# Up-projection of a conv feed-forward block: every product in three split products, with GpSimd making three quarters of the low weights

## Chip, core and metric

The kernel runs on one core of a Trainium2 chip. The metric is the device time of one launch in microseconds (us). All data are fp32. The core's engines are named as the profile names them: PE is TensorE (matmul), PEld its weight loads, DVE is VectorE, ACT is ScalarE, POOL is GpSimd, SP is the engine that issues most of the transfers.

## What is computed

The program is one block of a network on 256 tokens with 1024 features, followed by two layers of a second kind. The change is in the feed-forward part of the first block, in its up-projection:

```python
def conv_ffn(h, w_up_l, w_dwc_l, w_down_l, on_grid):
    p = h @ w_up_l                                  # 256 x 1024 times 1024 x 5632
    val, gate = p[..., :D_FF], p[..., D_FF:]        # D_FF = 2816
    ...
        gate = lax.conv_general_dilated(gate.reshape(bsz, rows, GRID_W, D_FF), w_dwc_l[:, :, None, :], ...)
    ...
    return (jax.nn.silu(gate) * val) @ w_down_l
```

The convolution is depthwise with nine taps on a 4 x 64 grid of tokens.

## The kernel before

Weights come as a stream of chunks of 128x2048 numbers (1 MB), chunk n into slot n % 4 of `raw`. A product with full accuracy is made of three fast ones (`mm3`): a number is split into a high part (rounded to the type fp32r) and a low part (the number less its high part), and high x high, low x high and high x low are summed in PSUM. ACT makes the high weights (`w_hi`, by a copy), DVE the low ones (`w_lo`, by a subtraction of `w_hi` from `raw`), both double-buffered by n % 2.

The up-projection has 22 chunks (N_UP = 14 to 35), each the weights of one block of 128 features: the first 1024 columns of a chunk make the value half, the last 1024 the gate half. A step of the stage is one chunk, and `up_chunk` (L445) is PE's part of it. Its value half is eight plain fp32 products of `raw` and `h_up` (L450; the profile counts each as two MATMULs), its gate half is 8 x 3 split products (L397 to L399). So only the gate half needs `w_hi` and `w_lo`. The order of the work is written out by hand on every engine, with semaphores:

- PE waits for `lo_ready` of the chunk and for a free PSUM bank (`evicted`; four banks, so PE may be up to three chunks ahead), and raises `chunk_done`.
- ACT (`up_steps` from L1374): copies the gate half out of PSUM twice (`gpad` L1378, `gacc` L1380), raises `gate_in`, makes the high gate weights of the chunk two further on (`prep`, 128x1024 from L1109), then a tanh of the chunk before (L1395) and the high part of the gated result of two chunks before (`mid_hi` L1400).
- DVE (`up_steps`): eight taps of the convolution (L2087), each waiting for the one before it, and between them two low-weight pieces of 512 columns (L2097) after the second and third tap, `mid_lo` (L2059), and the two steps of silu times value (L2064, L2069; the second reads the value half in PSUM and raises `evicted`). The ninth tap is in ACT's `gacc`.
- In the last two steps all 2048 columns of the first down-projection chunks are prepared, in four DVE pieces.
- GpSimd issues transfers of other weights (L362) and does nothing else.

Before the first chunk, DVE, ACT and PE go through the eight blocks of the normalised input: DVE scales (L2048), ACT adds the shift into `h_up` (L1370) and copies its high part (L1372), DVE subtracts (L2049).

Of the kernel before, what the change touches and what calls it, by code (L numbers as in the profile page):

```python
# [16 lines left out]
P = 128  # L17
D = 1024
KT = D // P
# [71 lines left out]
def build_program(nc, io, layers=LAYERS):  # L91
# [6 lines left out]
    with ctx:  # L98
# [9 lines left out]
        def at(name, shape, offset, dt=f32):  # L108
            return nc.alloc_sbuf_tensor_at(name, shape, dt, offset=offset)
# [51 lines left out]
        def S(name):  # L161
            if name not in sems:
                sems[name] = ctx.enter_context(nc.semaphore(name))
            return sems[name]
# [78 lines left out]
        mod_rows = at("mod_rows", [P, CH], F[0])  # L243
        ada_first = [ada_f[:, i, :] for i in range(4)] + [ada_a[:, i, :] for i in range(3)] + [ada_6[:, 0, :]]
        y1 = at("y1", [P, KT, T], A[5])
        h_up = at("h_up", [P, KT, T], F[2])

        mid_hi1 = at("mid_hi1", [P, FB, T], A[0], f32r)
        mid_lo1 = at("mid_lo1", [P, FB, T], A[0] + FB * T * 4, f32r)
# [103 lines left out]
        @block.gpsimd  # L353
        def _(pool):
            pool.wait_ge(S(f"ada_first{ADA_FIRST - 1}"), 16)

            def load(i, free=None):

                for c in range(2):
                    if free is not None:  # L360
                        pool.wait_ge(S("ada_used"), 2 * free + c + 1)
                    pool.dma_start(ada_home(i, c), io["ada"][2 * i + c + ADA_FIRST]).then_inc(ada_sem(i, c), 16)  # L362
            load(0)
            for i in range(1, 15):
                load(i, i - 1)
            load(15, 13)
            load(16, 14)
            load(17, 15)
            load(18, 16)
            pool.wait_ge(S("chunk_done"), N_DOWN)  # L370
            load(19, 17)
            load(20, 18)
            pool.wait_ge(S("chunk_done"), N_LAYER)
            load(21, 19)
            pool.wait_ge(S("gated"), 12)
            load(22, 20)
            load(23, 21)
            load(24, 22)
            load(25, 23)
            load(26, 24)  # L380
            pool.wait_ge(S("chunk_done"), N_LAYER + L_WOUT + 4)
            load(27, 25)
            load(28, 26)
            load(29, 27)
            pool.wait_ge(S("gated"), 24)
            load(30, 28)
            load(31, 29)
# [5 lines left out]
        def _(pe):  # L393
            mm, tr = nc.tensor.matmul, nc.tensor.transpose

            def mm3(out, ah, al, bh, bl, first, last, shared=False):
                mm(out, ah, bh, start=first, stop=False, skip_group_check=shared)  # L397
                mm(out, ah, bl, start=False, stop=False, skip_group_check=shared)  # L398
                return mm(out, al, bh, start=False, stop=last, skip_group_check=shared)  # L399
# [42 lines left out]
                                   act_hi[s][:, k, :], act_lo[s][:, k, :], k + b == 0, k == KT - 1, shared=True)  # L442
                return last

            def up_chunk(wp, slot, bank, m=None):  # L445

                for k in range(KT):
                    if m is not None:
                        pe.wait_ge(S("up_h"), k + 1)
                    mm(ps[:, bank, 0:T], raw[:, slot, k * P:(k + 1) * P], h_up[:, k, :], start=k == 0, stop=k == KT - 1)  # L450
                for k in range(KT):
                    if m is not None:
                        pe.wait_ge(S("mod_lo"), 8 * m + k + 1)
                    o = (KT + k) * P
                    last = mm3(ps[:, bank, T:2 * T], w_hi[:, wp, o:o + P], w_lo[:, wp, o:o + P],
                               act_hi[1][:, k, :], act_lo[1][:, k, :], k == 0, k == KT - 1)
                return last

            def tok_chunk(wp, bank, s):
# [425 lines left out]
            def up(i, m):  # L885
                for c in range(m):
                    first = isinstance(i, int) and i == 0
                    pe.wait_ge(S("lo_ready"), i + (N_UP + c + 1))
                    pe.wait_ge(S("evicted"), J_UP if first else i + (J_UP + c - 3))
                    more = {"m": 2} if first and c == 0 else {}  # L890
                    up_chunk((N_UP + c) % 2, (N_UP + c) % RAW, c % 4, **more).then_inc(S("chunk_done"), 1)
            up(0, 4)
            with pe.Fori(1, FB // 4) as i:
                up(i * 4, 4)
# [199 lines left out]
        def _(act):  # L1094
# [270 lines left out]
            root(2)  # L1365
            prep(N_OUT1 + 5, (N_OUT1 + 5) % RAW, (N_OUT1 + 5) % 2)
            norm_x(3, x, norm_sq1, 1)
            for b in range(KT):
                act.wait_ge(S("mod_pre"), 16 + b + 1)
                act_(h_up[:, b, :], norm_h1[:, b, :], ACT.Identity, bias=mod[:, 24 + b:25 + b]).then_inc(S("up_h"), 1)  # L1370
                act.wait_ge(S("up_h"), b + 1)
                act_(act_hi[1][:, b, :], h_up[:, b, :], ACT.Copy).then_inc(S("mod_hi"), 1)  # L1372

            def up_steps(i, c):  # L1374

                n, s, e, first = N_UP + c, c % 2, i + c, isinstance(i, int) and i == 0
                act.wait_ge(S("chunk_done"), i + (n + 1))
                act_(gpad[:, s, 1:ROWS + 1, 1:GRID_W + 1],  # L1378
                     ps[:, c % 4, T:2 * T].rearrange("p (r w) -> p r w", r=ROWS), ACT.Copy)
                act_(gacc[:, c, :], ps[:, c % 4, T:2 * T], ACT.Copy, scale=vec[:, bass.ds(e + (V1["dwc"] + 4 * FB), 1)])\  # L1380
                    .then_inc(S("gate_in"), 1)
                if isinstance(i, int):
                    prep(i + n + 2, (i + n + 2) % RAW, (i + n) % 2, CH // 2 if i + c + 2 < FB else 0)
                else:
                    prep((i + (n + 2), i * (16 // RAW) + ((n + 2) // RAW * 16 + 16)), (n + 2) % RAW, n % 2, CH // 2)
                if not (first and c == 0):
                    up_tanh(i, c)
                if not (first and c < 2):
                    up_mid(i, c)

            def up_tanh(i, c):

# [4 lines left out]
            def up_mid(i, c):  # L1397

                act.wait_ge(S("evicted"), i + (J_UP + c - 1))
                act_(mid_hi1[:, bass.ds(i + (c - 2), 1), :], gm[:, c % 2:c % 2 + 1, :], ACT.Copy).then_inc(S("mid_hi"), 1)  # L1400
# [242 lines left out]
        def _(dve):  # L1643
# [383 lines left out]
            for hf in (1, 0):  # L2027
# [18 lines left out]
            prep(N_UP + 1, (N_UP + 1) % RAW, (N_UP + 1) % 2)  # L2046
            root_done(3)
            pipe(2, lambda b: stt(norm_h1[:, b, :], x[:, b, :], gs[:, 1, b:b + 1], rstd[:, :], ALU.mult, ALU.mult),  # L2048
                 lambda b: tt(act_lo[1][:, b, :], h_up[:, b, :], act_hi[1][:, b, :].bitcast(f32), ALU.subtract))  # L2049
            nc.vector.memset(gpad[:, :, :, :], 0.0).then_inc(S("cleared"), 1)  # L2050
            order(nc.vector.memset(sw_wide[:, :, 8:16], 0.0))
            base = order.n
# [18 lines left out]
            def up_steps(i, c):  # L2071


                n, s, e, first = N_UP + c, c % 2, i + c, isinstance(i, int) and i == 0
                order.n = base if first and c == 0 else i * UP_MARKS + (base + c * UP_MARKS - 1)
                w_slot, r_slot = n % 2, (n + 2) % RAW
                gate_only = not isinstance(i, int) or i + c + 2 < FB
                pieces = {1: 1024, 2: 1536} if gate_only else {1: 0, 2: 512, 3: 1024, 4: 1536}
                dve.wait_ge(S("gate_in"), e + 1)
                acc = gacc[:, c, :].rearrange("p (r w) -> p r w", r=ROWS)  # L2080
                silu_mark = None
                for at_, tap in enumerate((0, 1, 2, 3, 5, 6, 7, 8)):
                    src = gpad[:, s, tap // 3:tap // 3 + ROWS, tap % 3:tap % 3 + GRID_W]
                    w = vec[:, bass.ds(e + (V1["dwc"] + tap * FB), 1)]
                    if at_:
                        dve.wait_ge(S("dve_order"), tap_mark)
                    ins = stt(acc, src, w, acc, ALU.mult, ALU.add)  # L2087
                    if at_ < 7:
                        order.mark(ins)
                        tap_mark = order.n  # L2090
                    else:
                        ins.then_inc(S("gconv"), 1)
                    if at_ in pieces:
                        if at_ == 1:
                            dve.wait_ge(S("hi_ready"), i + (n + 3))
                        o = slice(pieces[at_], pieces[at_] + 512)
                        ins = tt(w_lo[:, w_slot, o], raw[:, r_slot, o], w_hi[:, w_slot, o].bitcast(f32), ALU.subtract)  # L2097
                        if pieces[at_] == 1536:
                            ins.then_inc(S("lo_ready"), 1)
                    if at_ == 4 and not (first and c < 2):  # L2100
                        up_lo(e, s)
                    if not (first and c == 0):
                        if at_ == 5:
                            up_silu_a(e, 1 - s, (c + 3) % 4)
                            silu_mark = order.n
                        if at_ == 6:
                            up_silu_b(1 - s, (c + 3) % 4, silu_mark)
# [38 lines left out]
            for L in range(layers):  # L2146
# [265 lines left out]
                for hf in range(2):  # L2412
# [14 lines left out]
                        prep(n + c + 2, (n + c + 2) % RAW, (n + c) % 2)  # L2427
                        mlp_steps(0, c)
                    mlp_steps(0, 7)
                    prep_halves(n + 9, 2 * L + hf + 1)  # L2430
                    if hf == 1:
                        mods_out()
                    if hf == 0:
# [151 lines left out]
```

## Time and profile before

| | |
|---|---|
| Median of 3 runs | 1735.22 us (1732.3 to 1739.69) |
| The profiled execution: its own time | 1738.21 us |
| The profiled execution: span from the first to the last instruction | 1736.4 us |
| PE busy | 1648.1 us, 95% |
| DVE busy | 1108.8 us, 64% |
| ACT busy | 813.8 us, 47% |
| POOL busy | 34.0 us, 2% |

The engines work side by side, and busy times of matmuls overlap each other, so a busy PE is not PE at its peak. The shares are means over stages with different limits; the stage of the change lies between 327 and 482 us of the span.

### The profile page before, as it was taken

What the parts mean: (1) busy time and instruction counts of PE and PEld (TensorE: products, weight loads), DVE (VectorE), ACT (ScalarE), POOL (GpSimd) and SP (SyncE); (2) the same over time, 40 slices, a digit from 0 to 9 for tenths busy, and PEclk for the clock granted to TensorE, in tenths of its full rate; (3) what the DMA queues carried; (4) which work ended last, traced back from release to release, by engine and by line L of the source; (5) the groups of instructions that cost most, each with busy time, mean ns of one, the idle gap of its engine ahead of it and who ended that gap; (6) DMA issues with size and microseconds to landing.
All of it is one profiled execution on the core that took longest, in us unless ns stands there. A gap on an engine that the chain in (4) does not pass through costs nothing.

```text
span 1736.4 us, 34270 instructions
## 1 busy us (share of the span) xinstructions
PE 1648.1 (95%) x15182; PEld 1570.4 (90%) x15182; DVE 1108.8 (64%) x1400; ACT 813.8 (47%) x1057; POOL 34.0 (2%) x68
## 2 busy tenths in 40 slices
PE   5998999999998999999998999999999999989997
PEld 4996888799996999999997999979999999979996
DVE  3577744788946464678867545565546877665464
ACT  3346324433334536458544435444544675445352
POOL 0001000000000000000001000000000000000000
PEclk8999999999998999999999999999999999999998
DMA  9437444744546546445558655554454545735552
GB/s 390 159 123 264 151 178 180 269 166 165 203 175 229 170 147 194 157 170 182 173 193 346 235 189 194 188 208 171 151 189 146 195 170 175 267 117 193 193 189 81
DMA packets 45529, 331.40 MB, mean 191 GB/s; under 512 B 5072, under 2 KB 5072, under 8 KB 5456
## 3 DMA queue, kind: packets, MB, share of 16 engines
q1 hardware_dynamic: 36032, 260.73, 43.6%
q0 software_dynamic: 9216, 67.11, 9.9%
q8 instruction: 113, 1.85, 0.4%
q10 hardware_dynamic: 144, 1.51, 0.2%
q14 instruction: 24, 0.20, 0.0%
HBM read 326.18 MB, written 1.05 MB: 188 GB/s over the span
## 4 chain that ended last, share of the span: by engine, by line
PE 74%; DVE 12%; ACT 8%; DMA 4%; issue 2%; SPq 1%; POOL 0%; ACTq 0%; DVEq 0%; POOLq 0%
PE ps L397 19%; PE ps L399 19%; PE ps L398 19%; DVE w_lo L1652 5%; PE ps L450 4%; ACT w_hi L1109 4%; DMA raw<-stream 2%; PE ps L525 2%; DMA ada_alt<-ada 1%; PE ps L693 1%; PE ps L682 1%; DVE rsq L2420 1%; DMA ada_raw<-ada 1%; DVE rstd L1699 1%; PE ps L501 1%
## 5 line engine op out<-in xcount | busy, mean ns | idle before, releaser
L397 PE MATMUL ps<-act_hi,w_hi 128*128 128x256 f32 x2672 | 756.7, 283 | 17.6 <-DVE act_lo L1728 4.6
L1652 DVE TENSOR_TENSOR w_lo<-raw,w_hi 128x2048 fp32r<-128x2048 f32 x207 | 474.4, 2292 | 448.9 <-ACT w_hi L1109 448.3
L398 PE MATMUL ps<-act_lo,w_hi 128*128 128x256 f32 x2672 | 747.6, 280 | 0.0
L399 PE MATMUL ps<-act_hi,w_lo 128*128 128x256 f32 x2672 | 747.4, 280 | 0.0
L1109 ACT ACTIVATE w_hi<-raw 128x2048 fp32r<-128x2048 f32 (+1 forms) x229 | 421.8, 1842 | 513.4 <-PE ps L399 496.1
L397 PEld LDWEIGHTS ps<-act_hi,w_hi 128*128 128x128 f32 x2672 | 506.2, 189 | 24.7 <-issue 13.6
L398 PEld LDWEIGHTS ps<-act_lo,w_hi 128*128 128x128 f32 x2672 | 507.6, 190 | 0.7
L399 PEld LDWEIGHTS ps<-act_hi,w_lo 128*128 128x128 f32 x2672 | 506.3, 189 | 0.0
L397 PE MATMUL ps<-mlp_hi,w_hi 128*128 128x256 f32 x512 | 141.8, 277 | 0.4
L398 PE MATMUL ps<-mlp_lo,w_hi 128*128 128x256 f32 x512 | 141.4, 276 | 0.0
L399 PE MATMUL ps<-mlp_hi,w_lo 128*128 128x256 f32 x512 | 141.4, 276 | 0.0
L397 PEld LDWEIGHTS ps<-mlp_hi,w_hi 128*128 128x128 f32 x512 | 96.1, 188 | 1.0 <-DVE w_lo L1660 1.0
L398 PEld LDWEIGHTS ps<-mlp_lo,w_hi 128*128 128x128 f32 x512 | 96.2, 188 | 0.0
L399 PEld LDWEIGHTS ps<-mlp_hi,w_lo 128*128 128x128 f32 x512 | 96.1, 188 | 0.0
L2087 DVE SCALAR_TENSOR_TENSOR gacc<-gpad,vectors,gacc 128x256 f32<-128x256 f32 x176 | 84.7, 482 | 15.7 <-ACT gacc L1380 10.4
L450 PE MATMUL ps<-h_up,raw 128*128 128x256 f32 x352 | 80.4, 380 | 0.3
L450 PEld LDWEIGHTS ps<-h_up,raw 128*128 128x128 f32 x352 | 64.9, 190 | 9.8 <-ACT h_up L1370 1.5
L397 PE MATMUL ps<-w_hi,act_hi 128*128 128x256 f32 x256 | 72.5, 283 | 0.0
L399 PE MATMUL ps<-w_hi,act_lo 128*128 128x256 f32 x256 | 71.6, 280 | 0.0
L398 PE MATMUL ps<-w_lo,act_hi 128*128 128x256 f32 x256 | 71.4, 279 | 0.0
L1613 ACT ACTIVATE mlp_hi<-rsq 128x512 fp32r<-128x512 f32 x32 | 20.3, 633 | 73.0 <-DVE rsq L2420 73.0
L397 PE MATMUL ps<-mid_hi,w_hi 128*128 128x256 f32 x176 | 50.3, 286 | 3.3 <-DVE w_lo L1652 2.4
(442 smaller groups left out, 1991.9 us busy)
## 6 DMA issues: line engine op xcount, KB each, us to landing
raw<-stream SPq DMA_DIRECT2D x233, 1024.0 KB, 4.9
ada_raw<-ada POOLq DMA_DIRECT2D x46, 1024.0 KB, 6.6
ada_alt<-ada POOLq DMA_DIRECT2D x12, 1024.0 KB, 12.0
ada_f<-ada POOLq DMA_DIRECT2D x6, 1024.0 KB, 8.8
ada_f<-ada SPq DMA_DIRECT2D x4, 1024.0 KB, 15.0
ada_a<-ada SPq DMA_DIRECT2D x3, 1024.0 KB, 20.8
s<-s SPq DMA_DIRECT2D x4, 512.0 KB, 10.1
consts_stage<-consts_a SPq DMA_DIRECT2D x1, 1728.0 KB, 33.1
```

The lines of the kernel that those rows point to most:

```text
L397: mm(out, ah, bh, start=first, stop=False, skip_group_check=shared)
L398: mm(out, ah, bl, start=False, stop=False, skip_group_check=shared)
L399: return mm(out, al, bh, start=False, stop=last, skip_group_check=shared)
L450: mm(ps[:, bank, 0:T], raw[:, slot, k * P:(k + 1) * P], h_up[:, k, :], start=k == 0, stop=k == KT - 1)
L501: last = mm(ps[:, 7, 0:T], omean, sq[:, b, :], start=b == 0, stop=b == KT - 1)
L525: last = mm(ps[strip:strip + 32, bank, c * T:(c + 1) * T], cs_wide[:, k, 32 - 3 * j:64 - 3 * j], ada_home(i, c)[:, k * T:(k + 1) * T], sta ...
L682: last = mm(ps[r:r + 64, INV_BANK[q], j * 64:(j + 1) * 64], B01[d][r:r + 64, t0 + j // 4, j % 4, r:r + 64], Tm[r:r + 64, q, j, :], start=T ...
L693: last = mm(ps[r:r + 64, INV_BANK[q], j * 32:(j + 1) * 32], Uc[r:r + 64, q, j, :], half(X[r:r + 64, q, j, :], d, 1 << lvl), start=True, st ...
L1109: act_(w_hi[:, s2, o:CH], raw[:, s4, o:CH], ACT.Copy).then_inc(S("hi_ready"), 1)
L1613: act_(mlp_hi[:, bass.ds((i + c) * 2, 2), :], rsq[:, s, :].rearrange("p (b t) -> p b t", b=2), ACT.Copy)\
L1652: tt(w_lo[:, s2, :], raw[:, s4, :], w_hi[:, s2, :].bitcast(f32), ALU.subtract).then_inc(S("lo_ready"), 1)
L2087: ins = stt(acc, src, w, acc, ALU.mult, ALU.add)
```

## The change

The value half is made of split products too, so all 2048 columns of a chunk get high and low parts, and `h_up` goes. ACT makes the high weights in two halves, with a semaphore after each (`half_hi`, `hi_ready`). GpSimd subtracts columns 0 to 1023 after the first and 1024 to 1535 after the second; DVE keeps columns 1536 to 2047. PE waits for GpSimd's first piece ahead of the value half, and for its second piece and `lo_ready` ahead of the gate half. In the first chunk PE takes both halves block by block as the input's low parts arrive.

```diff
+            half, three = CH // 2, CH // 4 * 3
+            for e in range(2, FB):
+                n = N_UP + e
+                hi, lo, src = w_hi[:, n % 2, :].bitcast(f32), w_lo[:, n % 2, :], raw[:, n % RAW, :]
+                pool.wait_ge(S("half_hi"), e - 1 + 0)
+                nc.gpsimd.tensor_tensor(lo[:, 0:half], src[:, 0:half], hi[:, 0:half], ALU.subtract).then_inc(S("lo_pool"), 1)
+                pool.wait_ge(S("hi_ready"), n + 1)
+                nc.gpsimd.tensor_tensor(lo[:, half:three], src[:, half:three], hi[:, half:three], ALU.subtract).then_inc(S("lo_pool"), 1)
             pool.wait_ge(S("chunk_done"), N_DOWN)
...
-            def up_chunk(wp, slot, bank, m=None):
-
-                for k in range(KT):
-                    if m is not None:
-                        pe.wait_ge(S("up_h"), k + 1)
-                    mm(ps[:, bank, 0:T], raw[:, slot, k * P:(k + 1) * P], h_up[:, k, :], start=k == 0, stop=k == KT - 1)
-                for k in range(KT):
...
+            def up_chunk(wp, bank, n, lo):
+
+                for b in range(2):
+                    if lo is not None:
+                        pe.wait_ge(S("lo_pool"), lo + b)
+                    if b == 1:
+                        pe.wait_ge(S("lo_ready"), n + 1)
+                    for k in range(KT):
+                        o = (b * KT + k) * P
+                        last = mm3(ps[:, bank, b * T:(b + 1) * T], w_hi[:, wp, o:o + P], w_lo[:, wp, o:o + P],
+                                   act_hi[1][:, k, :], act_lo[1][:, k, :], k == 0, k == KT - 1)
                 return last
...
-            for b in range(KT):
-                act.wait_ge(S("mod_pre"), 16 + b + 1)
-                act_(h_up[:, b, :], norm_h1[:, b, :], ACT.Identity, bias=mod[:, 24 + b:25 + b]).then_inc(S("up_h"), 1)
-                act.wait_ge(S("up_h"), b + 1)
-                act_(act_hi[1][:, b, :], h_up[:, b, :], ACT.Copy).then_inc(S("mod_hi"), 1)
+            mod_hi(2, norm_h1, mod[:, 24:32], act_hi[1])
...
+            def up_prep(n, s4, s2):
+
+                act.wait_ge(S(f"raw_loaded{s4}"), n[1])
+                act.wait_ge(S("chunk_done"), n[0] - 1)
+                act_(w_hi[:, s2, 0:CH // 2], raw[:, s4, 0:CH // 2], ACT.Copy).then_inc(S("half_hi"), 1)
+                act_(w_hi[:, s2, CH // 2:CH], raw[:, s4, CH // 2:CH], ACT.Copy).then_inc(S("hi_ready"), 1)
...
-                pieces = {1: 1024, 2: 1536} if gate_only else {1: 0, 2: 512, 3: 1024, 4: 1536}
+                pieces = {2: 1536} if gate_only else {1: 0, 2: 512, 3: 1024, 4: 1536}
```

DVE's program, the start of one step of the loop over chunks, before. `gacc` is the running sum of the convolution, `gpad` the padded gate half; ISA and REGISTER_ALU rows are waits and address registers.

```order
L2087 ISA [waits gate_in]
L2087 SCALAR_TENSOR_TENSOR gacc<-gpad,vectors,gacc 128x256
L2086 ISA
L2087 ISA [waits dve_order]
L2087 SCALAR_TENSOR_TENSOR gacc<-gpad,vectors,gacc 128x256
L2095 REGISTER_ALU
L2097 TENSOR_TENSOR w_lo<-raw,w_hi 128x512 [waits hi_ready]
L2086 REGISTER_ALU
L2087 ISA [waits dve_order]
L2087 SCALAR_TENSOR_TENSOR gacc<-gpad,vectors,gacc 128x256
L2097 TENSOR_TENSOR w_lo<-raw,w_hi 128x512
```

The same place in the change:

```order
L2103 ISA [waits gate_in]
L2103 SCALAR_TENSOR_TENSOR gacc<-gpad,vectors,gacc 128x256
L2102 ISA
L2103 ISA [waits dve_order]
L2103 SCALAR_TENSOR_TENSOR gacc<-gpad,vectors,gacc 128x256
L2102 REGISTER_ALU
L2103 ISA [waits dve_order]
L2103 SCALAR_TENSOR_TENSOR gacc<-gpad,vectors,gacc 128x256
L2111 REGISTER_ALU
L2113 TENSOR_TENSOR w_lo<-raw,w_hi 128x512 [waits hi_ready]
```

One piece of 512 columns is gone, so the third tap now follows the second directly; the other piece and its wait on ACT stand after the third tap.

GpSimd's program around the stage, before: transfers only, and the one of `ada_f` waits until the whole up-projection is done.

```order
L362 DMA ada_raw<-ada 128x2048 [waits ada_used] x2
L362 DMA ada_alt<-ada 128x2048 [waits ada_used] x2
L362 DMA ada_f<-ada 128x2048 [waits ada_used,chunk_done]
L362 DMA ada_f<-ada 128x2048 [waits ada_used]
L362 DMA ada_raw<-ada 128x2048 [waits ada_used] x2
```

The change, at the same place; the last two rows stand there 20 times.

```order
L361 DMA ada_alt<-ada 128x2048 [waits ada_used] x2
L361 DMA ada_raw<-ada 128x2048 [waits ada_used] x2
L374 ISA
L374 TENSOR_TENSOR w_lo<-raw,w_hi 128x1024 [waits half_hi]
L376 TENSOR_TENSOR w_lo<-raw,w_hi 128x512 [waits hi_ready]
```

Forty subtractions and one other instruction are put between transfers that already waited for the stage's end.

## Rows read from the trace of the kernel before

**Rows 1.** The page: busy time of the engines over the whole span.

```profile
PE 1648.1 (95%) x15182; PEld 1570.4 (90%) x15182; DVE 1108.8 (64%) x1400; ACT 813.8 (47%) x1057; POOL 34.0 (2%) x68
```

**Rows 2.** Windows: length; busy PE, PEld, DVE, ACT, POOL (instructions); clock, DMA, GB/s.

```profile
400.00:469.00 69.00, 68.94 (x442) 64.15 (x440) 61.81 (x142) 26.20 (x56) 0.00 (x0) 1.00 0.50 168
```

**Rows 3.** Line L1378: count, shortest/median/longest, first and last start.

```profile
L1378 ACT ACTIVATE gpad<-ps x22: 385/386/388, 337.6 to 469.0; 128x256 f32<-128x256 f32 x22
```

**Rows 4.** Timeline of PE, one chunk: start us, us, what.

```profile
406.24 3.61 PE L450 MATMUL ps<-h_up,raw 128*128 128x256 f32 x16
409.50 0.47 PE L397 MATMUL ps<-act_hi,w_hi 128*128 128x256 f32 x1
409.81 0.28 PE L398 MATMUL ps<-act_lo,w_hi 128*128 128x256 f32 x1
...
412.43 3.61 PE L450 MATMUL ps<-h_up,raw 128*128 128x256 f32 x16
```

**Rows 5.** Timeline of ACT: high weights of whole split chunks in a later stage.

```profile
703.62 1.92 ACT L1109 ACTIVATE w_hi<-raw 128x2048 fp32r<-128x2048 f32 x1 [1.14 <-PE ps L399]
709.06 1.92 ACT L1109 ACTIVATE w_hi<-raw 128x2048 fp32r<-128x2048 f32 x1 [3.04 <-PE ps L399]
```

**Rows 6.** Timeline of DVE, one step of the stage.

```profile
407.33 1.11 DVE L2087 SCALAR_TENSOR_TENSOR gacc<-gpad,vectors,gacc 128x256 f32<-128x256 f32 x2 [0.35 <-ACT gacc L1380]
408.36 0.68 DVE L2097 TENSOR_TENSOR w_lo<-raw,w_hi 128x512 fp32r<-128x512 f32 x1
408.96 0.48 DVE L2087 SCALAR_TENSOR_TENSOR gacc<-gpad,vectors,gacc 128x256 f32<-128x256 f32 x1
409.36 0.69 DVE L2097 TENSOR_TENSOR w_lo<-raw,w_hi 128x512 fp32r<-128x512 f32 x1
...
412.78 0.48 DVE L2087 SCALAR_TENSOR_TENSOR gacc<-gpad,vectors,gacc 128x256 f32<-128x256 f32 x1
413.52 0.48 DVE L2087 SCALAR_TENSOR_TENSOR gacc<-gpad,vectors,gacc 128x256 f32<-128x256 f32 x1 [0.26 <-ACT gacc L1380]
```

**Rows 7.** Waits of DVE from 338 to 470 us: total, times, longest.

```profile
DVE gacc L2087 <- ACT gacc L1380: 10.4, 20, 2.5
```

**Rows 8.** Timeline of ACT, the same step.

```profile
406.44 0.39 ACT L1378 ACTIVATE gpad<-ps 128x256 f32<-128x256 f32 x1 [3.98 <-PE ps L399]
407.08 1.06 ACT L1109 ACTIVATE w_hi<-raw 128x1024 fp32r<-128x1024 f32 x1
408.02 0.42 ACT L1395 ACTIVATE gth<-gacc 128x256 f32<-128x256 f32 x1
```

**Rows 9.** Timeline at the stage's start, and the same preparation in a later stage.

```profile
327.04 1.28 DVE L2048 SCALAR_TENSOR_TENSOR norm_h<-x,gain_scale,rstd 128x256 f32<-128x256 f32 x3
328.89 1.07 PE L525 MATMUL ps<-ada_alt,silu_c_wide 128*32 128x256 f32 x16 [1.40 <-DMA ada_alt<-ada]
337.59 0.39 ACT L1378 ACTIVATE gpad<-ps 128x256 f32<-128x256 f32 x1 [3.14 <-PE ps L399]
552.81 1.28 DVE L1722 SCALAR_TENSOR_TENSOR s<-x,gain_scale,rstd 128x256 f32<-128x256 f32 x3
557.96 1.27 DVE L1723 SCALAR_TENSOR_TENSOR act_lo<-s,mod,act_hi 128x256 fp32r<-128x256 f32 x3
```

**Rows 10.** Lines: DVE's large and small low-weight subtractions, and GpSimd's only compute form.

```profile
L1652 DVE TENSOR_TENSOR w_lo<-raw,w_hi 128x2048 fp32r<-128x2048 f32 x207 | 474.4, 2292 | 448.9 <-ACT w_hi L1109 448.3
L2097 DVE TENSOR_TENSOR w_lo<-raw,w_hi 128x512 fp32r<-128x512 f32 x44 | 30.2, 686 | 0.8 <-ACT w_hi L1109 0.8
L2577 POOL MEMSET const-float32-1.0<- 128x1 f32 x1 | 0.1, 98 | 0.0
```

**Rows 11.** Tile gacc: the taps beside ACT's work (count, shortest/median/longest, first and last start).

```profile
L2087 DVE SCALAR_TENSOR_TENSOR gacc<-gpad,vectors,gacc x176: 475/482/488, 338.4 to 477.4; 128x256 f32<-128x256 f32 x176
```

**Rows 12.** Windows around a gap of PE in the stage that follows.

```profile
481.00:484.00 3.00, 0.65 (x6) 0.44 (x4) 2.28 (x2) 2.96 (x3) 0.00 (x0) 1.00 0.43 104
484.00:490.00 6.00, 5.94 (x31) 5.94 (x32) 2.29 (x2) 0.19 (x1) 0.00 (x0) 0.57 0.30 126
```

More of the change, by code:

```diff
@@ L245, in build_program @@
         y1 = at("y1", [P, KT, T], A[5])
-        h_up = at("h_up", [P, KT, T], F[2])
         mid_hi1 = at("mid_hi1", [P, FB, T], A[0], f32r)
@@ L443, in mod_chunk @@
                 return last
-            def up_chunk(wp, slot, bank, m=None):
-                for k in range(KT):
-                    if m is not None:
-                        pe.wait_ge(S("up_h"), k + 1)
-                    mm(ps[:, bank, 0:T], raw[:, slot, k * P:(k + 1) * P], h_up[:, k, :], start=k == 0, stop=k == KT - 1)
-                for k in range(KT):
[L452 to L456, printed above, removed]
+            def up_chunk(wp, bank, n, lo):
[8 more added lines that the diff above has]
+                                   act_hi[1][:, k, :], act_lo[1][:, k, :], k == 0, k == KT - 1)
                 return last
@@ L887, in up @@
                     first = isinstance(i, int) and i == 0
-                    pe.wait_ge(S("lo_ready"), i + (N_UP + c + 1))
+                    if first and c < 2:
+                        pe.wait_ge(S("lo_ready"), N_UP + c + 1)
                     pe.wait_ge(S("evicted"), J_UP if first else i + (J_UP + c - 3))
-                    more = {"m": 2} if first and c == 0 else {}
-                    up_chunk((N_UP + c) % 2, (N_UP + c) % RAW, c % 4, **more).then_inc(S("chunk_done"), 1)
+                    if first and c == 0:
+                        mod_chunk(N_UP % 2, 0, 1, 2).then_inc(S("chunk_done"), 1)
+                    else:
+                        lo = None if first and c < 2 else i * 2 + (2 * c - 3)
+                        up_chunk((N_UP + c) % 2, c % 4, i + (N_UP + c), lo).then_inc(S("chunk_done"), 1)
             up(0, 4)
@@ L1381, in up_steps @@
                     .then_inc(S("gate_in"), 1)
-                if isinstance(i, int):
-                    prep(i + n + 2, (i + n + 2) % RAW, (i + n) % 2, CH // 2 if i + c + 2 < FB else 0)
+                if not isinstance(i, int):
+                    up_prep((i + (n + 2), i * (16 // RAW) + ((n + 2) // RAW * 16 + 16)), (n + 2) % RAW, n % 2)
+                elif i + c + 2 < FB:
+                    up_prep((i + n + 2, (i + n + 2) // RAW * 16 + 16), (i + n + 2) % RAW, (i + n) % 2)
                 else:
-                    prep((i + (n + 2), i * (16 // RAW) + ((n + 2) // RAW * 16 + 16)), (n + 2) % RAW, n % 2, CH // 2)
+                    prep(i + n + 2, (i + n + 2) % RAW, (i + n) % 2)
                 if not (first and c == 0):
@@ L2048, in _ @@
             pipe(2, lambda b: stt(norm_h1[:, b, :], x[:, b, :], gs[:, 1, b:b + 1], rstd[:, :], ALU.mult, ALU.mult),
-                 lambda b: tt(act_lo[1][:, b, :], h_up[:, b, :], act_hi[1][:, b, :].bitcast(f32), ALU.subtract))
+                 lambda b: stt(act_lo[1][:, b, :], norm_h1[:, b, :], mod[:, 24 + b:25 + b], act_hi[1][:, b, :].bitcast(f32),
+                               ALU.add, ALU.subtract))
             nc.vector.memset(gpad[:, :, :, :], 0.0).then_inc(S("cleared"), 1)
@@ L2093, in up_steps @@
                     if at_ in pieces:
-                        if at_ == 1:
+                        if at_ == min(pieces):
                             dve.wait_ge(S("hi_ready"), i + (n + 3))
@@ L2429, in _ @@
                     mlp_steps(0, 7)
-                    prep_halves(n + 9, 2 * L + hf + 1)
+                    prep_halves(n + 9, FB - 2 + 2 * L + hf + 1)
                     if hf == 1:
```

## Prediction

> **What bounds the kernel now.** I read the page first: PE is busy 95% of the span, DVE 64%, ACT 47%, POOL 2% [rows 1]. These are means, so the stage of the change has to be read by itself. In the windows of the stage the picture differs: of 69 us PE is busy 68.9 and DVE 61.8, so DVE is nearly full as well, and POOL does nothing [rows 2]. ACT's first copy of the gate half starts 22 times between 337.6 and 469.0 us, 21 steps of (469.0 - 337.6) / 21 = 6.26 us [rows 3]. That is the step all below is measured against.
>
> PE's timeline shows what fills a step: the plain value half from 406.24 to 409.50, 3.26 us, and the split gate half from there to 412.43, 2.93 us, with nothing idle between [rows 4]. PE sets the pace. DVE's timeline shows how close it is behind: its eight taps run from 407.33, the last starts at 412.78, and another instruction could follow 0.40 us later (the spacing of the third tap and the piece behind it, 408.96 to 409.36), so a step of DVE is 413.18 - 407.33 = 5.85 us, and it then waits for ACT's `gate_in`, 0.26 to 0.35 us [rows 6]. Over the stage these waits are 10.4 us in 20 times [rows 7]. ACT has room: its chain of a step starts at 406.44 and is at its tanh at 408.02 [rows 8].
>
> **The change, part by part.** *PE.* Eight plain products go, 24 split ones come. In a later stage with chunks of 48 split products ACT starts on successive chunks 703.62 and 709.06, and it had waited for PE: 5.44 us for a chunk [rows 5]. So PE needs 5.45 us where it took 6.26, 0.8 less. That is the whole of what the change can gain in a step.
>
> *DVE.* One piece of 512 columns goes: from 408.36 to 408.96, 0.60 us [rows 6]. The third tap now stands right behind the second, on which it waits. The first two taps show what that costs: they span 1.11 us and a tap lasts 0.48, so the second began 0.63 after the first, 0.23 more than the 0.40 of a neighbour that needn't wait [rows 6]. DVE's step is 5.85 - 0.60 + 0.23 = 5.48 us, the same as PE's. So DVE has no room left; whatever lengthens it moves the step.
>
> *ACT.* The high weights double to two copies of 128x1024. One takes 408.02 - 407.08 = 0.94 us of the queue [rows 8], and the work that hides the second is PE's chunk: ACT waits 3.98 us a step for PE now [rows 8]. Behind the second copy the tanh starts 0.94 us later, at about 2.7 us into a step; DVE asks for it in the middle of its next step. Nothing. `hi_ready` comes about 0.1 us after DVE would ask for it at its third tap when DVE starts at once on `gate_in`: 0.07 us, so that I use 5.55 us for a step that nothing else disturbs.
>
> *GpSimd.* A step adds subtractions of 128x1024 and 128x512. The trace has no such instruction on this engine; its only compute rows are fills of one column at 98 ns [rows 10]. The nearest rows are DVE's own subtractions, 2292 ns for 2048 columns and 686 for 512 [rows 10]: (2292 - 686) / 1536 = 1.05 ns a column and 0.15 fixed. At that price the pair takes 1.9 us, the lower bound; at double the price 3.8, which I take as the upper. I choose 3.5: both operands read one after the other double the part per column, 2 x 1.05 x 1.536 + 2 x 0.15. Either fits beside a step of 5.5 us, and the first piece would be ready 1.8 (ACT) + 2.3 = 4.1 us after a `chunk_done`, ahead of PE's need at 5.45. By length alone GpSimd is hidden. The Trainium skill has a price (GPSIMD Engine Reference, § 3.1): 4497 ns for 2048 columns on GpSimd against 2293 on VectorE; the trace agrees on the second (2292). By it the pair takes 3.4 us instead of 3.5 and the sum below is 2 us less. The lone other instruction ahead of GpSimd's first subtraction, of unknown cost, has from the end of the transfers' release near 327 us to the first `half_hi` near 338, and is free up to that.
>
> *Whether GpSimd and DVE work side by side* is the question, because DVE is full. Nearly all of DVE's step reads two SBUF operands, and so does GpSimd's pair. Below, they don't touch each other, and DVE's step stays 5.55. Above, one stands still while the other reads: then 5.48 + 3.5, less about 0.3 for GpSimd's work that falls in DVE's own pauses of 0.23 behind a tap, 8.7 us. A gain needs DVE to lose less than 0.7 us to a pair of 3.5, a fifth of it; of the interval from 5.55 to 8.7 three quarters lie above 6.26. For the lower end speaks that the taps beside ACT's work stay between 475 and 488 ns [rows 11]; but no ACT instruction there reads two operands. I take the upper end as the likeliest, at even odds against all others together. The Trainium skill has a rule that speaks against this change (SBUF — State Buffer, § Who interferes with whom): VectorE's second SBUF operand comes through a read interface shared with GpSimd, and the later of the two "fully blocks" until the other is done. By it the step is about 8.6 us. No run here shows it yet.
>
> *Start of the stage.* ACT no longer makes `h_up`. A later stage prepares its eight blocks in the way that the change does: from 552.81 to 557.96 + 1.27, 6.4 us [rows 9]. From 327.04 on that ends at 333.5. PE is busy with another product until 328.89 + 1.07 = 329.96 and then needs 5.45 for its chunk: 335.4. Now the first copy behind the first chunk starts at 337.59 [rows 9], some 0.2 after the chunk's end: 2.0 us gained.
>
> *The end.* The last two steps keep their four DVE pieces; the first down-projection chunk follows DVE in both, so that the end moves with DVE.
>
> **The sum.** 20 steps carry GpSimd's pair: 20 x (8.7 - 6.26) = 48.8, less 2.0: +47 us on the profiled execution's own 1738.2, 1785. The median of the runs lies 3.0 below that execution, so 1782. With the pair at 1.9 us the step is 7.1, +15 and 1750; at 3.8 and nothing in pauses 9.28, +58 and 1794. One more cost may come on top: behind a gap of 2.4 us in PE's work the granted clock was 0.57 over 6 us, near the lower of its levels, 1.2 GHz [rows 12]. With PE waiting 3 us in each step its products would run partly at that level; half-rate 48 products take 10.9 us, more than a step, so a low clock closes the gap by which it came. I allow 0.5 us a step for it at the top, 1804.
>
> **Rivals.** *Free side by side* (0.29): DVE's and GpSimd's reads don't meet. Step 5.55, 20 x 0.71 + 2.0 = 16 us gained, 1722 on the profiled execution, 1719 for the median, 1715 to 1724. For it: the undisturbed taps beside ACT. It decides where DVE loses under 0.7 us a step. *Shared, not blocked* (0.17): both go on at less than full rate, DVE's step between 6.2 and 8.0; from -2 to +33 us, 1733 to 1767. For it: GpSimd needs the reads for part of the time only, if its price is above DVE's. Against it nothing in the trace. *GpSimd itself too slow* (0.04): a pair that costs over 6.26 us, such as four times DVE's price, 7.6, makes PE wait for `lo_pool`: 20 x 1.4 - 2 = +25, 1760. Against it: it is twice my upper bound. *Blocked* (0.50) is the forecast, its own range 1750 to 1804.
>
> **The numbers.** The likeliest case gives 1782. To leave out no more than 2 in 10 the range must reach the free case: 1715 to 1805. Half a per cent, about what a measurement can tell here from no change, is 8.7 us: below 1726.5 is faster, which is the free case and a little over, 0.30; the low end of the shared case is no change, 0.05; the rest is slower, 0.65.
>
> **What would show it.** In the profile after: the spacing of ACT's gate copies (8.7, or 5.55); the taps of DVE (482 ns now) with some of 1 to 2.5 us where a GpSimd subtraction runs, or a spacing of the taps that grows as much; GpSimd's durations near 2.3 and 1.2 us; PE waiting about 3 us a step for DVE's `lo_ready` or GpSimd's `lo_pool`; the first gate copy at 335.6; PE's split chunk at 5.45 us at full clock. The prediction is wrong if the taps keep their 0.40 and 0.63 us while GpSimd subtracts, if GpSimd's pair costs far from 3.5 us, or if PE's clock falls and stays down.

## The result, and the profile after

The change makes the kernel slower: 1776.93 us median (1775.73 to 1779.99, 4 runs) where the kernel before takes 1737.45 (1732.3 to 1746.2, 4 runs). The ratio is 1.0214, 95% interval 1.0181 to 1.0247. The forecast was 1782, on the profiled execution's own scale 1785; that execution took 1779.99 us. Here and below times are medians of all runs, while the ratios leave out two outliers: 1743.84 us, one of the ten runs with operands from PSUM, and 1865.39 us, one of the 27 of the kernel before beside the later experiments.

The page of the profile after, busy time of the engines, beside [rows 1]:

```profile
PE 1653.3 (93%) x15358; PEld 1580.7 (89%) x15358; DVE 1157.5 (65%) x1380; ACT 830.5 (47%) x1069; POOL 112.6 (6%) x108
```

DVE executes 20 instructions fewer and is busy 49 us longer. The timeline of DVE, one step and the start of the next, answers to [rows 6]:

```profile
399.88 2.13 DVE L2103 SCALAR_TENSOR_TENSOR gacc<-gpad,vectors,gacc 128x256 f32<-128x256 f32 x4
401.93 0.68 DVE L2113 TENSOR_TENSOR w_lo<-raw,w_hi 128x512 fp32r<-128x512 f32 x1
402.53 3.01 DVE L2103 SCALAR_TENSOR_TENSOR gacc<-gpad,vectors,gacc 128x256 f32<-128x256 f32 x2
405.46 1.51 DVE L2075 TENSOR_TENSOR mid_lo<-gm,mid_hi 128x256 f32 x1
406.89 0.47 DVE L2103 SCALAR_TENSOR_TENSOR gacc<-gpad,vectors,gacc 128x256 f32<-128x256 f32 x1
...
408.35 2.31 DVE L2103 SCALAR_TENSOR_TENSOR gacc<-gpad,vectors,gacc 128x256 f32<-128x256 f32 x4
```

And the timeline of GpSimd over the same time (the bracket is the idle time before and what ended it):

```profile
402.78 2.47 POOL L374 TENSOR_TENSOR w_lo<-raw,w_hi 128x1024 fp32r<-128x1024 f32 x1 [4.56 <-ACT w_hi L1403]
405.22 1.47 POOL L376 TENSOR_TENSOR w_lo<-raw,w_hi 128x512 fp32r<-128x512 f32 x1
411.24 2.68 POOL L374 TENSOR_TENSOR w_lo<-raw,w_hi 128x1024 fp32r<-128x1024 f32 x1 [4.56 <-ACT w_hi L1403]
```

The two are to be laid on each other. A step now takes 408.35 - 399.88 = 8.47 us. Two taps in a row that took 1.11 us [rows 6] take 3.01, from 402.53 to 405.54, while GpSimd's first subtraction runs (402.78 to 405.25); the next instruction, `mid_lo`, takes 1.51 while the second runs. Undisturbed they take 1.11 and 0.42, as in the step of the same trace that follows GpSimd's last pair:

```profile
504.58 1.11 DVE L2103 SCALAR_TENSOR_TENSOR gacc<-gpad,vectors,gacc 128x256 f32<-128x256 f32 x2
505.60 0.42 DVE L2075 TENSOR_TENSOR mid_lo<-gm,mid_hi 128x256 f32 x1
```

The loss is 1.90 + 1.09 = 2.99 us, and 8.47 - 2.99 = 5.48, the step of DVE that the prediction worked out. Everything else in the step keeps its duration.

The wait of PE, from 338 to 510 us (total, times, longest):

```profile
PE ps L404 <- DVE gm L2085: 35.8, 18, 2.9
```

PE, which had no gap in the stage [rows 2], now waits for the instruction that raises `evicted`: it runs ahead until it has no free PSUM bank, and then goes at DVE's pace. The window of one step (length; busy PE, PEld, DVE, ACT, POOL; clock, DMA, GB/s) shows DVE as the full engine and the clock at 0.80:

```profile
399.88:408.35 8.47, 7.37 (x48) 7.18 (x48) 8.04 (x14) 3.26 (x6) 3.91 (x2) 0.80 0.19 78
```

The clock falls to its lower level for part of this chunk, which stands behind a wait of 2.74 us. In PE's timeline its products follow each other every 0.12 us, then every 0.21, then every 0.11, and the chunk is nevertheless done 1.09 us before PE can go on; the next chunk, behind that shorter wait, has no such stretch:

```profile
400.09 0.38 PE L404 MATMUL ps<-act_hi,w_hi 128*128 128x256 f32 x1 [2.74 <-DVE gm L2085]
400.30 0.28 PE L405 MATMUL ps<-act_lo,w_hi 128*128 128x256 f32 x1
400.42 0.28 PE L406 MATMUL ps<-act_hi,w_lo 128*128 128x256 f32 x1
...
402.76 0.41 PE L406 MATMUL ps<-act_hi,w_lo 128*128 128x256 f32 x1
402.98 0.41 PE L404 MATMUL ps<-act_hi,w_hi 128*128 128x256 f32 x1
...
408.56 0.38 PE L404 MATMUL ps<-act_hi,w_hi 128*128 128x256 f32 x1 [1.09 <-DVE gm L2085]
```

Over more steps GpSimd's first subtraction starts 402.78 and, eleven steps on, 496.34 in this row of its timeline, 8.51 us a step:

```profile
496.34 2.49 POOL L374 TENSOR_TENSOR w_lo<-raw,w_hi 128x1024 fp32r<-128x1024 f32 x1 [4.55 <-ACT w_hi L1403]
```

So 20 x (8.51 - 6.26) = 45 us, less what the start of the stage gains (below, 1.8): 43, an estimate that takes all 20 steps as alike. The two profiled executions differ by 41.8.

### The profile page after: what moved, and what is told of

Its sections match the earlier page's. It is cut to its first block, busy times and chain, and to the rows that moved or that the text cites. A ratio compares the mean times of both kernels' runs of the same rounds, so it can differ in the third digit from the quotient of the medians.

```text
span 1778.2 us, 34688 instructions
## 1 busy us (share of the span) xinstructions
PE 1653.3 (93%) x15358; PEld 1580.7 (89%) x15358; DVE 1157.5 (65%) x1380; ACT 830.5 (47%) x1069; POOL 112.6 (6%) x108
## 3 DMA queue, kind: packets, MB, share of 16 engines
q10 hardware_dynamic: 144, 1.51, 0.2%
HBM read 326.18 MB, written 1.05 MB: 184 GB/s over the span
## 4 chain that ended last, share of the span: by engine, by line
PE 71%; DVE 14%; issue 6%; ACT 5%; DMA 4%; DVEq 0%; SPq 0%; POOL 0%; ACTq 0%; POOLq 0%
PE ps L404 19%; PE ps L406 19%; PE ps L405 19%; DVE gacc L2103 4%; DVE w_lo L1667 4%; ACT w_hi L1119 3%; PE ps L531 2%; DMA ada_alt<-ada 2%; PE ps L688 1%; PE ps L699 1%; PE ps L507 1%; DMA ada_raw<-ada 1%; DVE w_lo L2113 1%; DMA ada_f<-ada 1%; PE ps L1016 1%
## 5 line engine op out<-in xcount | busy, mean ns | idle before, releaser
L404 PE MATMUL ps<-act_hi,w_hi 128*128 128x256 f32 x2848 | 809.1, 284 | 52.2 <-DVE gm L2085 35.8
L406 PE MATMUL ps<-act_hi,w_lo 128*128 128x256 f32 x2848 | 802.4, 282 | 0.0
L405 PE MATMUL ps<-act_lo,w_hi 128*128 128x256 f32 x2848 | 802.3, 282 | 0.0
L1119 ACT ACTIVATE w_hi<-raw 128x2048 fp32r<-128x2048 f32 x209 | 400.5, 1917 | 512.3 <-PE ps L406 501.8
L404 PEld LDWEIGHTS ps<-act_hi,w_hi 128*128 128x128 f32 x2848 | 545.7, 192 | 62.8 <-issue 49.5
L406 PEld LDWEIGHTS ps<-act_hi,w_lo 128*128 128x128 f32 x2848 | 545.9, 192 | 0.0
L405 PEld LDWEIGHTS ps<-act_lo,w_hi 128*128 128x128 f32 x2848 | 545.6, 192 | 0.1
L2103 DVE SCALAR_TENSOR_TENSOR gacc<-gpad,vectors,gacc 128x256 f32<-128x256 f32 x176 | 124.0, 712 | 9.9 <-ACT gacc L1386 2.1
L361 POOL DMA_DIRECT2D ada_raw<-ada x46 | 24.4, 531 | 1328.2 <-DVE s L2386 735.8
L374 POOL TENSOR_TENSOR w_lo<-raw,w_hi 128x1024 fp32r<-128x1024 f32 x20 | 50.1, 2505 | 91.6 <-ACT w_hi L1403 91.6
```

The source lines that it names most:

```text
L374: nc.gpsimd.tensor_tensor(lo[:, 0:half], src[:, 0:half], hi[:, 0:half], ALU.subtract).then_inc(S("lo_pool"), 1)
L1119: act_(w_hi[:, s2, o:CH], raw[:, s4, o:CH], ACT.Copy).then_inc(S("hi_ready"), 1)
```

## The experiments

The theory: an instruction of DVE that reads two SBUF operands stands still while GpSimd reads its own, and the other way round. The rivals: any work of GpSimd in SBUF stops DVE; a loss for each GpSimd instruction; the longer chain of waits, ACT's second copy or the clock sets the step. All kernels are the change with the edit shown, timed beside the kernel before, which took 1741 us in these rounds.

**GpSimd's pair cut to 8 columns each.**

```diff
-nc.gpsimd.tensor_tensor(lo[:, 0:half], src[:, 0:half], hi[:, 0:half], ALU.subtract) ...
+nc.gpsimd.tensor_tensor(lo[:, 0:8], src[:, 0:8], hi[:, 0:8], ALU.subtract) ...
```

(The second one alike. Dots stand for code that is not shown.)

> GpSimd's two subtractions of the change are cut to 8 columns each, with all waits, semaphores, high weights in halves and split products as they are; the low weights of 1520 columns of a chunk are left out. Theory (VectorE's instructions stand still while GpSimd reads its operands): the step falls from 8.45 to about 5.55 us, 20 x 2.9 = 58 us less than the change: about 1720 us, 1% under the kernel before. Rival (the longer chain of waits, ScalarE's second copy or TensorE's lower clock set the step): stays at 1765 to 1780.

Measured: 1724.62 us, ratio 0.990 (0.9852 to 0.9947). The tap row of DVE by lines (count, busy, mean ns, idle before) is back at [rows 11]:

```profile
L2103 DVE SCALAR_TENSOR_TENSOR gacc<-gpad,vectors,gacc 128x256 f32<-128x256 f32 x149 | 71.3, 482 | 8.1 <-ACT gacc L1386 0.7 <-DVE gacc L2103 0.3
```

Every wait, semaphore and copy of the change is still there, so the chain of waits is not the cause. The length of GpSimd's work is.

**GpSimd writes and does not read.**

```diff
-nc.gpsimd.tensor_tensor(lo[:, 0:half], src[:, 0:half], hi[:, 0:half], ALU.subtract) ...
+for r in range(2):
+    nc.gpsimd.memset(lo[:, 0:half].bitcast(f32), 0.0).then_inc(S("lo_pool"), 1)
+    pool.wait_ge(S("lo_pool"), 6 * (e - 2) + r + 1)
+nc.gpsimd.memset(lo[:, 0:half].bitcast(f32), 0.0).then_inc(S("lo_pool"), 1)
...
```

(The second one alike; PE's waits count three fills for each piece.)

> GpSimd fills the same columns three times over with zeros in place of each subtraction: it writes as many columns and more, and is busy for some 2.5 to 4 us a step, but reads nothing. The low weights of these columns are left out. Theory (what collides is the reading of two SBUF operands): about 1720, taps of VectorE at 482 ns. Rival (any GpSimd access to SBUF stops VectorE): 1750 to 1780, with taps of 1 us and more beside the fills.

Measured: 1722.38 us, ratio 0.9898 (0.9851 to 0.9946). Lines, GpSimd's fills and DVE's taps beside them:

```profile
L375 POOL MEMSET w_lo<- 128x1024 f32 x38 | 36.4, 958 | 16.6 <-ACT w_hi L1409 15.5
...
L380 POOL MEMSET w_lo<- 128x512 f32 x38 | 19.9, 524 | 1.1
```

```profile
L2109 DVE SCALAR_TENSOR_TENSOR gacc<-gpad,vectors,gacc 128x256 f32<-128x256 f32 x153 | 72.4, 481 | 7.8 <-ACT gacc L1392 0.3 <-DVE gacc L2109 0.3
```

Three fills of each kind are 4.4 us of GpSimd in a step, more than the pair of subtractions, and DVE's taps stay at 481 ns. GpSimd at work does DVE no harm as long as it only writes.

**GpSimd reads one operand.**

```diff
-nc.gpsimd.tensor_tensor(lo[:, 0:half], src[:, 0:half], hi[:, 0:half], ALU.subtract) ...
+nc.gpsimd.tensor_copy(lo[:, 0:half], src[:, 0:half]) ...
```

(The second one alike.)

> GpSimd copies the raw weights in place of subtracting: one SBUF operand read, the same columns written; the low weights of these columns are replaced by the raw ones. Theory: VectorE stands still for as long as the copies read; if a copied column costs half of a subtracted one (2.04 ns by the change's 2505 and 1460 ns), the pair takes 2 us and the step is 5.48 + 1.6 = 7.1: about 1750. Rival (only two operands against two operands collide): about 1720.

Measured: 1735.11 us, ratio 0.9952 (0.9927 to 0.9976), between the two. GpSimd's and DVE's timelines:

```profile
408.71 1.16 POOL L374 CAST w_lo<-raw 128x1024 fp32r<-128x1024 f32 x1 [4.53 <-ACT w_hi L1403]
409.81 0.80 POOL L376 CAST w_lo<-raw 128x512 fp32r<-128x512 f32 x1
```

```profile
408.48 1.66 DVE L2103 SCALAR_TENSOR_TENSOR gacc<-gpad,vectors,gacc 128x256 f32<-128x256 f32 x2
410.06 0.82 DVE L2075 TENSOR_TENSOR mid_lo<-gm,mid_hi 128x256 f32 x1
```

The same two places stretch, 1.66 for 1.11 and 0.82 for 0.42: 0.95 us lost to copies of 1.96. One operand is enough to collide, so the rival that needs two against two is out. The expected 1.6 was too much: part of a copy falls into the tap already running and into the pause behind it, and with short copies that is half of them. In both places DVE's instruction ends 0.27 us after GpSimd's (410.14 and 409.87, 410.88 and 410.61), and in the change 0.29 and 0.28 us after (405.54 and 405.25, 406.97 and 406.69): about what its 256 columns take at 1.05 ns each [rows 10], as if it read only once GpSimd was done.

**DVE reads its second operand from PSUM.**

```diff
...
+src = ps[:, c % 4, T:2 * T].rearrange("p (r w) -> p r w", r=ROWS)
 ins = stt(acc, src, w, acc, ALU.mult, ALU.add)
...
-tt(mid_lo1[:, b, :], gm[:, s:s + 1, :], mid_hi1[:, b, :].bitcast(f32), ALU.subtract)
+tt(mid_lo1[:, b, :], ps[:, bank:bank + 1, 0:T], mid_hi1[:, b, :].bitcast(f32), ALU.subtract)
...
-order.mark(stt(gth[:, s, :], gth[:, s, :], 1.0, gacc[:, a, :], ALU.add, ALU.mult))
+order.mark(stt(gth[:, s, :], gth[:, s, :], 1.0, ps[:, bank, T:2 * T], ALU.add, ALU.mult))
```

> GpSimd as in the change; VectorE's eight taps, its low part of the gated result and its first silu step read one operand from PSUM (the chunk's own bank) in place of SBUF, so that only its 512-column piece of low weights still reads two SBUF operands. The convolution and the gate are changed by that. Theory (VectorE collides by its second SBUF operand): step 5.5 to 6, 1720 to 1732, with the one piece of 512 columns stretched where it meets GpSimd. Rival (GpSimd's reads stop every VectorE instruction, or the waits set the step): 1765 to 1780.

Measured: 1723.74 us, ratio 0.9901 (0.9873 to 0.9929). GpSimd's lines and DVE's, from 345 to 450 us:

```profile
L374 POOL TENSOR_TENSOR w_lo<-raw,w_hi 128x1024 fp32r<-128x1024 f32 x19 | 45.8, 2410 | 31.5 <-ACT w_hi L1403 31.5
L376 POOL TENSOR_TENSOR w_lo<-raw,w_hi 128x512 fp32r<-128x512 f32 x19 | 26.5, 1393 | 0.0
```

```profile
L2104 DVE SCALAR_TENSOR_TENSOR gacc<-ps,vectors,gacc 128x256 f32<-128x256 f32 x151 | 71.1, 479 | 7.5 <-DVE gacc L2104 0.3
L2114 DVE TENSOR_TENSOR w_lo<-raw,w_hi 128x512 fp32r<-128x512 f32 x20 | 16.6, 832 | 0.0
...
L2075 DVE TENSOR_TENSOR mid_lo<-ps,mid_hi 128x256 f32 x16 | 6.6, 414 | 0.0
```

GpSimd does all of its subtractions, and the 42 us are gone. Only the piece that still reads two SBUF operands is stretched, 832 ns in the mean for 686 [rows 10]. That mean comes from the first steps, where piece and subtractions meet and the piece takes up to 1.83 us; later they fall apart, the piece takes 0.68 us and GpSimd's small subtraction 1.30. With the fills this shows both sides: the collision is between DVE's second SBUF operand and GpSimd's reads.

**DVE makes all low weights.**

```diff
-pieces = {2: 1536} if gate_only else {1: 0, 2: 512, 3: 1024, 4: 1536}
+pieces = {1: 0, 2: 512, 3: 1024, 4: 1536}
```

(GpSimd's loop and PE's waits for it go; PE waits for `lo_ready` ahead of the value half.)

> The change without GpSimd: VectorE makes all low weights in four pieces of 512 columns between its taps, the rest as in the change. Theory (a column given to GpSimd costs VectorE more than making it itself): the last two steps before had four such pieces and took about 6.7 us, so 20 x (6.7 - 6.26) - 2 = +7: about 1747 where the kernel before takes 1740, and some 30 us under the change. Rival (split products, the halves and their waits cost the time, not GpSimd): 1770 and more.

Measured: 1747.18 us, ratio 1.0036 (1.0016 to 1.0056), as expected. PE's wait and the window from 345 to 450 us:

```profile
PE ps L396 <- DVE w_lo L2105: 14.8, 15, 1.3
```

```profile
345.00:450.00 105.00, 90.36 (x754) 87.45 (x755) 102.75 (x231) 54.49 (x96) 0.00 (x0) 1.00 0.46 160
```

DVE is full with this, too, but the three more pieces cost it less than GpSimd's help: 30 us are to be had by sending GpSimd away.

**Half the columns.**

```diff
-...(lo[:, 0:half], src[:, 0:half], hi[:, 0:half], ALU.subtract) ...
+...(lo[:, 0:512], src[:, 0:512], hi[:, 0:512], ALU.subtract) ...
...
-...(lo[:, half:three], src[:, half:three], hi[:, half:three], ALU.subtract) ...
+...(lo[:, half:half + 256], src[:, half:half + 256], hi[:, half:half + 256], ALU.subtract) ...
```

> The change with GpSimd's pair cut to half its columns, 512 and 256; the low weights of the other 768 columns are left out. Theory: what VectorE loses goes with the columns, 2.04 ns each by the change's two durations: 768 x 2.04 = 1.57 us a step less, step 6.9, 20 x 1.57 = 31 us under the change: about 1748. Rival (a loss for each GpSimd instruction, whatever its length): 1775.

Measured: 1747.7 us, ratio 1.0021 (0.9999 to 1.0043), as expected. DVE's timeline has the same two places, shorter:

```profile
405.45 1.92 DVE L2103 SCALAR_TENSOR_TENSOR gacc<-gpad,vectors,gacc 128x256 f32<-128x256 f32 x2
407.29 0.95 DVE L2075 TENSOR_TENSOR mid_lo<-gm,mid_hi 128x256 f32 x1
...
412.27 1.92 DVE L2103 SCALAR_TENSOR_TENSOR gacc<-gpad,vectors,gacc 128x256 f32<-128x256 f32 x2
```

The step is 6.82 us and the loss 0.81 + 0.53 = 1.34 us; 768 columns fewer took 1.65 us off, 2.15 ns a column. The loss goes with the columns and not with the number of instructions.

**A version on this ground: all sums in PSUM.** It computes all that the kernel before does. The convolution's sum stays in the gate half's place in PSUM, the gated result in the value half's; then no DVE instruction of the 20 steps reads two SBUF operands, and GpSimd makes all 2048 columns. The tanh, the first silu step, `mid_hi` and `mid_lo` read from PSUM too (not shown in the diff). PE waits for `mid_ready` in place of `evicted`, as the bank is free later.

```diff
-act_(gacc[:, c, :], ps[:, c % 4, T:2 * T], ACT.Copy, scale=...)
+act_(ps[:, c % 4, T:2 * T], ps[:, c % 4, T:2 * T], ACT.Copy, scale=...)
...
-acc = gacc[:, c, :].rearrange("p (r w) -> p r w", r=ROWS)
+acc = ps[:, c % 4, T:2 * T].rearrange("p (r w) -> p r w", r=ROWS)
...
-stt(gm[:, s, :], gth[:, s, :], 0.5, ps[:, bank, 0:T], ALU.mult, ALU.mult)
+stt(ps[:, bank, 0:T], gth[:, s, :], 0.5, ps[:, bank, 0:T], ALU.mult, ALU.mult)
...
-half, three = CH // 2, CH // 4 * 3
+half, three = CH // 2, CH
...
-pieces = {2: 1536} if gate_only else {1: 0, 2: 512, 3: 1024, 4: 1536}
+pieces = {} if gate_only else {1: 0, 2: 512, 3: 1024, 4: 1536}
```

> A version built on the theory, with all of the computation: the convolution's sum stays in the gate half's place in PSUM and the gated result in the value half's place, so that every VectorE instruction of a step reads one SBUF operand; GpSimd makes all low weights, in two halves of 1024 columns. Theory: VectorE's step 4.9 to 5.1 us, GpSimd's 4.9, TensorE sets the pace at 5.45: 20 x 0.81 + 2 = 18 us under the kernel before, about 1722 where that takes 1740. Rival (GpSimd stops VectorE in another way as well, or GpSimd's longer work sets the step): 1740 and more.

Measured: 1725.58 us, ratio 0.9899 (0.9869 to 0.9928): faster than the kernel before by 1%, than the change by 3%. The window and GpSimd's lines:

```profile
345.00:450.00 105.00, 105.00 (x894) 105.00 (x893) 84.47 (x201) 60.25 (x112) 88.23 (x38) 1.00 0.54 182
```

```profile
L376 POOL TENSOR_TENSOR w_lo<-raw,w_hi 128x1024 fp32r<-128x1024 f32 x19 | 45.7, 2405 | 0.0
```

GpSimd works 88 of 105 us and DVE 84, beside each other, and PE has no gap.

**The same with the change's shares,** GpSimd's three quarters and one DVE piece with two SBUF operands (`half, three` and `pieces` as in the change).

> As the version with sums in PSUM, but with GpSimd's three quarters and VectorE's piece of 512 columns as in the change, so that one VectorE instruction of a step still reads two SBUF operands. Theory: that piece may meet a GpSimd subtraction and then takes up to 2.4 us more; if they meet, a step of 5.5 to 7; if they fall apart as they did with operands from PSUM alone, 5.45: 1722 to 1750, with the lower end likelier. Rival: 1765 to 1780.

Measured: 1734.15 us, ratio 0.9958 (0.993 to 0.9985): the one piece costs half of the gain, and the lower end was not the likelier. Timelines of GpSimd and of DVE, one step:

```profile
398.99 2.41 POOL L374 TENSOR_TENSOR w_lo<-raw,w_hi 128x1024 fp32r<-128x1024 f32 x1 [2.21 <-ACT w_hi L1406]
401.35 1.74 POOL L376 TENSOR_TENSOR w_lo<-raw,w_hi 128x512 fp32r<-128x512 f32 x1
```

```profile
400.40 1.54 DVE L2116 TENSOR_TENSOR w_lo<-raw,w_hi 128x512 fp32r<-128x512 f32 x1
```

The two meet, and each delays the other: the piece, begun within GpSimd's first subtraction, takes 1.54 us for 0.69 and ends at 401.94, 0.54 us after that subtraction; GpSimd's second, begun within the piece, takes 1.74 for the 1.30 above.

Two of the programs were run once more, one execution each, for the pace of PE; what came of it stands in the last section.

> The same program as the version with all sums in PSUM, looked at once more. In its first profile TensorE's split products followed each other every 0.118 us through the whole stage, in the runs with fills and with operands from PSUM every 0.113, at the same granted clock of 1.00. If the program sets the pitch, it is 0.118 again and the gate copies 5.65 us apart; if the execution sets it, it may be 0.113 and 5.44, and the time some 4 us less.

> The same program as the run in which GpSimd only fills, looked at once more (the low weights of these columns are left out). First profile: pitch 0.113 us, gate copies 5.43 us apart. If the program sets the pitch it is the same; if the execution sets it, it may be 0.118 and 5.65.

## Why the prediction was right

**The question it hung on, whether the two engines work side by side.** They do not, by the runs with fills and with PSUM operands. In the trace of the change the loss sits in two places of a step and not in a general slowing, and there DVE's instruction ends only when GpSimd's is done, so that the sharing rival falls, and the free one with it. The rule of the Trainium skill that was weighed (SBUF — State Buffer, § Who interferes with whom) holds here in both of its parts: the one that comes second waits, DVE's 0.42 us as long as 1.51 and GpSimd's 1.30 as long as 1.74 (in the version with the change's shares), and a GpSimd instruction that only writes does not count.

**The sizes.** GpSimd's pair was put at 3.5 us; alone it takes 2.41 + 1.30 = 3.7 in the run with PSUM operands. The Trainium skill's 4497 ns for 2048 columns (GPSIMD Engine Reference, § 3.1), which gave 3.4, is nearly met by the trace: 2 x 2405 = 4810 ns in two instructions. Of the pair 0.3 us were put into DVE's pauses; 2.99 are lost, so it is 0.7. The price was too low and the part that costs nothing too small, and that these two errors partly cancel is luck: 5.48 + 2.99 = 8.47 for the 8.7 forecast. DVE's undisturbed step of 5.48 came out to the hundredth, and the start gained 1.8 us for 2.0: in the trace after, the first scaling of the input starts at 329.77 and the first gate copy at 338.5, 8.7 us, where [rows 9] gave 10.55. One sum among the rivals is off by a microsecond: a step of 6.2 gives 20 x (6.2 - 6.26) - 2 = -3 us, not -2; nothing rests on it.

```profile
329.77 1.28 DVE L2063 SCALAR_TENSOR_TENSOR norm_h<-x,gain_scale,rstd 128x256 f32<-128x256 f32 x3
```

```profile
L1384 ACT ACTIVATE gpad<-ps x22: 364/367/387, 338.5 to 508.5; 128x256 f32<-128x256 f32 x22
```

**What was missed.** PE was to wait for `lo_ready` or `lo_pool`; it waits for `evicted`. The low weights were in time: GpSimd's pair that ends at 406.69 is for the chunk that PE starts at 408.56. DVE's lateness reaches PE by the banks that it frees. The waits are 35.8 us in 18 times, 2.0 us each where about 3 were forecast. The allowance for a low clock was not needed: PE's products do run at the lower level for part of a step, but a chunk at that pace, 7.4 us busy, still fits into 8.47. That no other part of the change costs anything was right: with 8 columns on GpSimd it gives the 1% that the free case promised.

## To carry to other kernels

Before work is handed to GpSimd, look at how many SBUF operands VectorE's instructions read beside it: here each column on GpSimd took 2.0 ns from VectorE, which makes the same column itself in 1.05. An operand moved to PSUM lifted the collision at no cost in duration (taps of 479 ns for 482). And with an engine that has 0.4 us of room in a step of 6.3, ask first what lengthens that engine, not how busy the helper is.

## What the runs showed of the hardware that was not expected

A blocked instruction of DVE shows in the trace as a longer one (3.01 us for two taps), not as a wait, so the list of waits does not name GpSimd at all; only the two timelines laid on each other do.

TensorE has two paces at the same granted clock. Where nothing held it, split products followed each other every 0.113 us or every 0.118, so that a chunk of 48 took 5.44 or 5.65 us. Gate copies in the run with fills and in the second run of the same program, 22 each:

```profile
L1390 ACT ACTIVATE gpad<-ps x22: 387/388/392, 338.9 to 453.0; 128x256 f32<-128x256 f32 x22
```

```profile
L1390 ACT ACTIVATE gpad<-ps x22: 385/386/390, 335.4 to 454.1; 128x256 f32<-128x256 f32 x22
```

114.1 / 21 = 5.43 and 118.7 / 21 = 5.65 us: the same program shows both, so the program does not set the pace. The version with all sums in PSUM kept to 5.65 us in its second run. Nor does the pace belong to a whole execution. In the second run with fills, two windows at a clock of 1.00, the second of them in the next stage, have 851 products in 100 us (0.118 each) and 356 in 40 us (0.112 each):

```profile
350.00:450.00 100.00, 100.00 (x851) 100.00 (x850) 91.74 (x215) 56.89 (x105) 77.38 (x107) 1.00 0.54 183
480.00:520.00 40.00, 40.00 (x356) 40.00 (x355) 19.04 (x19) 17.97 (x13) 0.00 (x0) 1.00 0.58 192
```

What sets it stays open. It is worth 4.6 us in this stage, but it does not account for the times: the run with fills took 1717.35 us with the slower pace in this stage and 1718.68 with the faster one, and the version with all sums in PSUM 1720.08 and 1727.09 us, both times with the slower. Why the unhindered versions have medians of 1722 to 1726 and not the 1720 expected is not shown.
